# A ring of 30 load buffers in place of 24 for the experts' weights, in another order

## The reference

```python
for l in range(2):
    h = modulate(rms_norm(x), shift1, scale1)
    proj = h @ w_in                       # conv, pool and gate inputs
    y_a = conv_branch(...)                # 31 taps, layer norm, silu, @ w_conv_out
    y_b = pool_branch(...)
    x = x + g1 * ((gate_a * y_a + gate_b * y_b) @ w_out)
    h2 = modulate(rms_norm(x), shift2, scale2)
    # 32 experts, top 2 within the best of 4 groups, D_EXPERT = 256
    x = x + g2 * moe(h2, w_router, w_expert_gate, w_expert_up, w_expert_down)
out = rms_norm(x)
```

## Time and profile before

| | us |
|---|---|
| median of 3 runs | 1653.76 |
| lowest and highest | 1653.06, 1659.18 |
| the profiled execution | 1658.35 |
| its span | 1656.6 |

### The profile page before, as it was taken

How to read it: one execution, slowest core, us unless ns; L and a number is a source line. 1 busy time by engine, 2 the same in 40 slices (tenths; PEclk the granted TensorE clock), 3 DMA queues, 4 the chain that set the end, 5 groups by cost and what they waited for, 6 DMA issues and landing times.

```text
span 1656.6 us, 27402 instructions
## 1 busy us (share of the span) xinstructions
PE 1512.8 (91%) x10609; PEld 1197.3 (72%) x10609; DVE 904.2 (55%) x1607; ACT 576.7 (35%) x916; POOL 3.7 (0%) x9
## 2 busy tenths in 40 slices
PE   9999999989789999999999999887879999888886
PEld 7999989989778898999989895222229888422222
DVE  6898887672454478888869764100118975300102
ACT  5544356423444644343451432111115143211101
POOL 0000000000000000000000000000000000000000
PEclk9999999999899999999989999999899999999998
DMA  8998845203423365888824368999994447899996
GB/s 309 380 355 306 286 150 177 94 26 137 169 77 103 115 223 200 312 303 306 294 68 150 106 240 321 409 409 410 409 407 146 140 153 267 321 409 409 409 409 252
DMA packets 115803, 420.87 MB, mean 254 GB/s; under 512 B 12945, under 2 KB 13089, under 8 KB 115569
## 3 DMA queue, kind: packets, MB, share of 16 engines
q1 hardware_dynamic: 114624, 414.19, 67.2%
q0 software_dynamic: 1072, 5.20, 0.9%
HBM read 416.71 MB, written 2.62 MB: 253 GB/s over the span
## 4 chain that ended last, share of the span: by engine, by line
PE 54%; DVE 15%; DMA 15%; SPq 7%; ACT 5%; issue 4%; DVEq 0%; ACTq 0%
PE work L856 20%; PE acc L856 11%; DMA over_select<-wstream_d 9%; SPq L683 7%; DVE yconv L2557 6%; DMA over_splits<-wstream_d 5%; PE work L947 5%; PE work L1490 2%; DVE wlo L2030 2%; PE work L816 2%; ACT whi L1580 2%; PE work L826 2%; PE work L891 2%; PE work L1425 1%; DMA ln_squares<-wstream_d 1%
## 5 line engine op out<-in xcount | busy, mean ns | idle before, releaser
L2030 DVE TENSOR_TENSOR wlo<-raw,whi 128x1024 fp32r<-128x1024 f32 x264 | 320.9, 1223 | 192.8 <-ACT whi L1580 192.4
L1580 ACT ACTIVATE whi<-raw 128x1024 fp32r<-128x1024 f32 x264 | 276.9, 1056 | 278.0 <-PE work L856 185.2
L856 PE MATMUL work<-hhi,whi 128*128 128x256 f32 x1024 | 293.1, 286 | 2.2 <-DVE hlo L2058 1.3
L856 PE MATMUL work<-hlo,whi 128*128 128x256 f32 x1024 | 291.7, 285 | 0.0
L856 PE MATMUL work<-hhi,wlo 128*128 128x256 f32 x1024 | 291.6, 285 | 0.0
L856 PEld LDWEIGHTS work<-hhi,whi 128*128 128x128 f32 x1024 | 198.5, 194 | 4.8 <-DVE wlo L2030 3.0
L856 PEld LDWEIGHTS work<-hlo,whi 128*128 128x128 f32 x1024 | 198.6, 194 | 0.1
L856 PEld LDWEIGHTS work<-hhi,wlo 128*128 128x128 f32 x1024 | 198.5, 194 | 0.0
L2767 DVE TENSOR_TENSOR pair_b<-work,pair_a 128x256 f32<-128x256 f32 x16 | 6.8, 425 | 240.2 <-ACT pair_a L1985 240.2
L1490 PE MATMUL work<-over_splits,xg 128*32 128x512 f32 x448 | 107.8, 603 | 16.4 <-DMA over_splits<-wstream_d 14.8
L2136 DVE SCALAR_TENSOR_TENSOR ada_tiles<-ada_tiles,c_act 128x1024 f32<-128x1024 f32 x96 | 116.3, 1219 | 0.9 <-DMA ada_tiles<-ada_d 0.9
(11 more groups left out here) (444 smaller groups left out, 2651.1 us busy)
## 6 DMA issues: line engine op xcount, KB each, us to landing
raw<-wstream_d SPq DMA_DIRECT2D x400, 512.0 KB, 4.6
over_splits<-wstream_d SPq DMA_DIRECT2D x128, 512.0 KB, 15.5
ada_tiles<-ada_d SPq DMA_DIRECT2D x96, 512.0 KB, 5.2
over_select<-wstream_d SPq DMA_DIRECT2D x64, 512.0 KB, 14.9
over_pool<-wstream_d SPq DMA_DIRECT2D x32, 512.0 KB, 15.4
spare_d<-wstream_d SPq DMA_DIRECT2D x32, 512.0 KB, 14.5
yconv<-wstream_d SPq DMA_DIRECT2D x16, 512.0 KB, 14.6
ln_squares<-wstream_d SPq DMA_DIRECT2D x16, 512.0 KB, 15.5
```

The costliest lines, as they stand in the source:

```text
L856: mm = pe.matmul(out, a, b, start=(start and k == 0), stop=(stop and k == n - 1), skip_group_check=skip)
L1580: act.activation(whi[n % AHEAD][:], tiles[SLOT[SPLITS[n]]][:], ACT.Copy).then_inc(s("hi_done"), 1)
L2030: dve.tensor_tensor(wlo[n % AHEAD][:], tiles[SLOT[SPLITS[n]]][:], whi[n % AHEAD][:].bitcast(F32), ALU.subtract).then_inc(s("lo_done"), 1)
```

## The change

The ring has 30 buffers. Six are added at its end: slot 24 is `over_acts` (the space of `ahi` and `alo`, last used in `ffn2`), 25 is `c_act` (last used there too), 26 `over_ppad`, 27 `over_vpad`, 28 and 29 the two halves of `hf`. The order becomes: slots 16 to 25, raw, `over_pool`, `over_splits`, and slots 26 to 29 last. The first load into slot 26 waits for `router_mm`, those into 27 to 29 for `router_read`. The loop has 5 turns of 30, and the last 12 tiles are written out. `vpad`'s and `ppad`'s zero margins, which were written once ahead of both layers, are now written in each layer, after the norm's scaling and before the conv inputs.

```diff
-RING = EXTRA + 8
+RING = EXTRA + 14
@@ ring(l)
-    out = [(first + j) % RAW for j in range(RAW)] + list(range(RAW, SIDE)) + list(range(EXTRA, RING))
+    out = list(range(EXTRA, RING - 4)) + [(first + j) % RAW for j in range(RAW)] + list(range(RAW, SIDE))
     for j in sorted(range(AHEAD), key=lambda j: last_split(l, j)):
         out += [SIDE + j, SIDE + AHEAD + j]
-    return out
+    return out + list(range(RING - 4, RING))
@@ buffers
-        ahi = sb("ahi", [P, 2, T], F32R)
-        alo = sb("alo", [P, 2, T], F32R)
+        acts = ExitStack()
+        ahi = sb("ahi", [P, 2, T], F32R, acts)
+        alo = sb("alo", [P, 2, T], F32R, acts)
+        acts.close()
+        over_acts = sb("over_acts", [P, TILE])
...
-        vpad = sb("vpad", [P, 4, 30 + T])
+        pads_only = ExitStack()
+        vpad = sb("vpad", [P, 4, 30 + T], F32, pads_only)
+        ppad = sb("ppad", [P, 4, 16 + T], F32, pads_only)
+        pads_only.close()
+        over_vpad = sb("over_vpad", [P, 4 * (30 + T)])[:, 0:TILE]
+        over_ppad = sb("over_ppad", [P, 4 * (16 + T)])[:, 0:TILE]
         yconv = sb("yconv", [P, 4, T])
-        ppad = sb("ppad", [P, 4, 16 + T])
...
-            t[:, :, :].rearrange("p c t -> p (c t)") for t in (yconv, ln_squares)]
+            t[:, :, :].rearrange("p c t -> p (c t)") for t in (yconv, ln_squares)] + [
+            over_acts, c_act, over_ppad, over_vpad, hf[:, 0:4, :].rearrange("p c t -> p (c t)"),
+            hf[:, 4:8, :].rearrange("p c t -> p (c t)")]
@@ load(r), first use of a slot
-                    if SLOT[r] >= EXTRA:
+                    if SLOT[r] >= RING - 4:
+                        sp.wait_ge(s("router_mm" if SLOT[r] == RING - 4 else "router_read"), l + 1)
+                    elif SLOT[r] >= EXTRA:
                         sp.wait_ge(s("pe_tile"), START[f"conv{l}"] + 4)
@@ SP, the experts' loop
-                    with sp.Fori(0, 6 * EXPERTS // RING - 1) as i:
+                    turns = 6 * EXPERTS // RING - 1
+                    with sp.Fori(0, turns) as i:
                         for j in range(RING):
                             load(r + j, i)
-                    r += 6 * EXPERTS - RING
+                    r += RING * turns
@@ DVE
-            dve.memset(vpad[:, :, 0:30], 0.0)
-            own(dve.memset(ppad[:, :, 0:16], 0.0))
             for l in range(LAYERS):
...
                     modulation(1)
+                dve.memset(vpad[:, :, 0:30], 0.0)
+                own(dve.memset(ppad[:, :, 0:16], 0.0))
```

## The result

| | kernel before | changed kernel |
|---|---|---|
| median | 1656.54 us (5 runs) | 1643.77 us (5 runs) |
| lowest and highest | 1653.06, 1659.18 | 1642.0, 1644.96 |
| span of the profiled execution | 1656.6 | 1643.2 |

The ratio is 0.9924, with a 95% interval of 0.9905 to 0.9943: faster by 12.6 us. The forecast was 15.1 us faster, with 1643.7 us as its upper end; the result lies on that edge, just outside. (The kernel before had shown 1653.76 us over 3 runs when the forecast was made; with two more its median is 1656.54.)

A forecast was written before the change was run, and what follows sets the result against it. Expert weight loads were taken to bound both layers' expert stages, after a gap with the ring full. Terms -15.4 + 0.3 = -15.1 us took the median from 1653.76 to 1638.7 us, range 1635.5 to 1643.7.

The forecast's parts named there:

- What bounds the kernel: Experts of both layers: loads at 407 to 410 GB/s bound them, with a full ring idling the DMA ahead of each.
- Six more buffers: Experts' stages: 30 tiles in place of 24 at PE's start, the last load 7.7 us earlier, twice: -15.4 us.
- the 30 land in time: Ahead of the experts: the last four loads land at 1007.5 us, 10 us early; if late, 5.1 us gain left.
- PE keeps up: Experts' stage: PE takes 0.69 us a tile against 1.28 for a load; cover 113 us against 7.7 us used.
- The change of layers: After the last expert tiles: a1's first two loads wait for tiles 190 and 191; +0.3 us once, bounds 0 and 1.3.
- Memsets, pairs, loop, loads beside wout0: Margin writes on DVE hidden (0.3 us uncovered); shared semaphores, five loop turns and earlier loads under wout0 products: nothing.
- The range: Whole kernel, median: 1635.5 to 1643.7 us, from 1.0 us for a1's late start, 0.3 for memsets, and run scatter.
- the three signs of being wrong: Plateau shorter by under 7 us a layer, its rate under 400 GB/s, or last-product-to-first-square gap up over 2 us.
- Rival B: a1's first tiles: their loads take 15.5 us in place of 3.3, ACT waits some 12 us; 1650 us; 2%.
- A: Ahead of the experts: last four buffers too late or PE's start moved, 5.1 us or less gained; about 1649; 4%.
- C: Expert loads lose rate with the new targets; at 380 GB/s 1.38 us a tile and 1671 us; 2%.
- D: First expert loads: a wait holds the first ten until the router, 28 us slower, at 1682; 1%.

The follow-up runs named there:

- mended order: The changed kernel's 30 buffers with over_pool ahead of the raw buffers in the order; 0.9897 and 0.9911 of the kernel before in two runs.

## Why the prediction was right or wrong

**What bounds the kernel: right.** The gap ahead of the plateau, the full ring and the loads as the bound are all as read; the order alone gave nothing, and depth gave about what a tile's load costs in the rings of 28, 30 and 32 (1.39, 1.26 and 1.34 us a tile, over two stages); the ring of 26 gave half.

**Six more buffers: right.** -15.4 us was forecast. The six profiles with 30 buffers have 15.1 us less in the two stages (429.7 against 444.8), the changed kernel's own three 15.7 us (429.1). That the 30 land in time, that PE keeps up and the rate of 409 GB/s, which the sum took from the rows instead of the 358 GB/s of the Trainium skill ("DMA: Bandwidth & Descriptors", Where 436 GB/s comes from), held too; 32 buffers show no sign of a lower rate.

**The change of layers: the step that failed.** The prediction called it "a dead heat" and put +0.3 us, with 1.3 us as its bound. It measured +3.2, +3.2 and +3.1 us. The place and the wait were named, the size was wrong by ten, in two ways:
- *The lateness* was 0.9 us (squares at 5.20 in place of 4.28 us) and up to 1.7 us. PE's end of tile 190 was taken from the old profile, 1.2 us ahead of the last product's end. In the new one the eight matmul records of tiles 190 and 191 run together in 1.57 us, and SP's issue comes only 0.5 us ahead of that end. The step moved the old timeline as a whole, although the products there were spaced by the very loads that now come sooner.
- *The clock* was left out: 2.1 us more in the sum of squares (4.85 to 6.95 us). A sum that starts 0.9 us later was priced as 0.9 us of delay. But the clock falls in this stretch in every profile, in the kernel before too, so a later start also puts 0.9 us less of the sum ahead of the fall, and that part then takes nearly twice as long (the whole sum took 3.62 and 3.70 us ahead of the fall, 6.95 us behind it): about 0.8 of the 2.1 us, an estimate from these figures. The ring of 24 with late tiles bears it out with a sum of 5.34 us. The other 1.3 us come from the fall itself, at 5.4 in place of 7.4 us after the last product. Filling the pause moved the fall to 11.0 us and brought the 2.1 us back; the lateness stayed.

Why the fall came early is open. In the changed kernel it came at 5.4, 7.6 and 5.2 us; without late tiles and with a short pause it came at 5.6 us (28 buffers) and at 7.6 and 6.0 us (mended order); with late tiles and the long pause in a ring of 24, at 7.8 us. So neither the late tiles nor the pause decide it alone. That all three stretches of the changed kernel are within 0.1 us of 17.5 is in part luck: in one of them the squares came 0.7 us later and the fall 2.2 us later.

**Memsets, pairs, loop, loads beside wout0:** nothing shows against them. The two memsets lie ahead of a wait of 3.76 us of DVE at the change of layers.

**The range** had 1.0 us for the change of layers above the forecast. With 3.2 us there the same sum is -12.2 us, near the measured 12.6; the mean of the three runs of this kernel is 10.8, and the 1.4 us between are left open. The agreement to 0.4 us is in part luck. The spans of the two profiles differ by 13.4 us: 0.7 more ahead of the experts, 8.2 less in their first stage, 3.2 more at the change of layers, 2.1 less from there to the second stage, 8.2 less in it, and 1.2 more in the tail. The 2.1 us are no gain of the change: that stretch takes 164.4 to 166.2 us in the profiles with 24 buffers and 164.0 to 166.6 us in those with 30. The rest is level: the median of before had been 1653.76 us and became 1656.54, so the changed kernel's time came out above the range although the difference misses by 2.5 us only. Of the three signs of being wrong that the prediction named none came: the stages fell by 8.2 us each, the rate was 406 GB/s, and the squares came 0.9 us later. It had no sign for the sum behind the squares. Rival B had the right place and a wrong mechanism, a load queued behind others; SP's queue was empty, as said. A, C and D did not occur.

## What to carry to other kernels

When a stage is bound by loads and a gap in the loads lies ahead of it, each further buffer filled in that gap is worth one load's time at the end; starting the same loads sooner is worth nothing. After changing a ring's length, work out which tiles hold, at its end, the buffers that the next stage loads first: 192 = 6 x 30 + 12 put the last two tiles just there, and a turned order gave 2.6 and 6.9 us back for nothing. And when work on TensorE near a fall of its clock is delayed, price the products behind the fall as well, at the lower level.

## What the runs showed that had not been expected

Filled pauses at one norm (sum 3.70 and 3.62 us) went with a final sum of 8.01 and 7.89 us, in both kernels that had them; in the second the dummy products inside the final sum are part of it, and no clear gain in time is left. In the experts' stage the clock is at the 1.2 GHz level for stretches while PE waits for loads; the stages' lengths show no charge for it except in the last ten microseconds of the ring of 26. And nearly 5 us of the difference between two executions of the kernel before lie ahead of the stages compared here, so that stages of a profile separate kernels which medians of five runs do not.

One thing stays untested. In the eight profiles with 30 or 32 buffers the first expert product is at 1014.1 to 1016.6 us; with 24, 26 or 28 it is at 1010.4 to 1012.4 us in four profiles and at 1015.5 and 1015.9 us in two. Whether the deeper rings cost something ahead of the experts, or this is the scatter of that part, these profiles do not tell.
